# Wide 512-column matmuls for seven query and key chunks, a later load of x and four fewer mask additions

## The reference

```python
def even_layer(x, g_norm, w_in, b_f, w_out):
    z = rms_norm(x, g_norm) @ w_in
    qa, ka, va, ga, fa, qb, kb, vb, gb = jnp.split(z, cuts, axis=-1)
    log_f = jax.nn.log_sigmoid(fa.astype(f32) + b_f.astype(f32))
    ya = forgetting_attention(hA(qa), hA(ka), hA(va), log_f).reshape(Bsz, S, WIDTH_FOX)
    yb = dilated_attention(hB(qb), hB(kb), hB(vb)).reshape(Bsz, S, WIDTH_DIL)
    y = jnp.concatenate([ya * jax.nn.silu(ga), yb * jax.nn.silu(gb)], axis=-1)
    return x + y @ w_out

def odd_layer(x, g_norm, w_in, w_out):
    z = rms_norm(x, g_norm) @ w_in
    q, k, v, g = jnp.split(z, [qk_w, 2 * qk_w, 2 * qk_w + v_w], axis=-1)
    q = rotate(q.reshape(Bsz, S, N_HEADS_RET, RET_QK_DIM))
    k = rotate(k.reshape(Bsz, S, N_HEADS_RET, RET_QK_DIM)) * (RET_QK_DIM ** -0.5)
    y = retention(q, k, v.reshape(Bsz, S, N_HEADS_RET, RET_V_DIM))
```

## Time and profile before

| | us |
|---|---|
| median of 3 runs | 771.15 (771.01 to 771.21) |
| the profiled execution | 770.69 |
| its span, first to last instruction | 768.9 |
| PE busy | 760.5 (99%) |
| DVE busy | 517.2 (67%) |
| ACT busy | 409.8 (53%) |
| POOL busy | 223.6 (29%) |
| DMA moved | 132.01 MB, mean 172 GB/s |

### The profile page before, as it was taken

How to read it: one execution, slowest core, us unless ns; L and a number is a source line. 1 busy time by engine, 2 the same in 40 slices (tenths; PEclk the granted TensorE clock), 3 DMA queues, 4 the chain that set the end, 5 groups by cost and what they waited for, 6 DMA issues and landing times.

```text
span 768.9 us, 12573 instructions
## 1 busy us (share of the span) xinstructions
PE 760.5 (99%) x5026; PEld 658.3 (86%) x5026; DVE 517.2 (67%) x779; ACT 409.8 (53%) x664; POOL 223.6 (29%) x176
## 2 busy tenths in 40 slices
PE   9999999999999999999999999999999999999997
PEld 8889987899877899987778888988888888888885
DVE  5876756665577558765567965778788676667553
ACT  6674458443696453353344554727857555456451
POOL 2110996730940000064029900126012111011010
PEclk9999999999999999999999999999999999999999
DMA  9999893588512746555435565430465556655751
GB/s 284 220 233 301 245 248 65 131 174 198 156 62 80 242 138 194 186 169 159 142 110 164 191 218 168 140 134 30 164 193 152 183 175 204 194 179 175 242 169 55
DMA packets 78490, 132.01 MB, mean 172 GB/s; under 512 B 4592, under 2 KB 28304, under 8 KB 78304
## 3 DMA queue, kind: packets, MB, share of 16 engines
q1 hardware_dynamic: 76928, 126.01, 55.7%
q0 software_dynamic: 1216, 5.09, 2.3%
q10 hardware_dynamic: 288, 0.11, 0.1%
HBM read 130.12 MB, written 1.06 MB: 171 GB/s over the span
## 4 chain that ended last, share of the span: by engine, by line
PE 97%; DVE 1%; ACT 1%; issue 0%; DVEq 0%; ACTq 0%
PE ps L1711 15%; PE ps L1715 15%; PE ps L1719 15%; PE ps L1769 10%; PE ps L1752 6%; PE ps L1756 6%; PE ps L1748 6%; PE ps L1777 5%; PE ps L1839 2%; PE ps L1855 2%; PE ps L1870 2%; PE ps L2225 1%; PE ps L2102 1%; PE ps L2054 1%; PE ps L2110 1%; PE ps L1799 1%
## 5 line engine op out<-in xcount | busy, mean ns | idle before, releaser
L1032 DVE TENSOR_TENSOR w_lo<-stage,w_hi 128x1024 fp32r<-128x1024 f32 x224 | 293.4, 1332 | 150.9 <-ACT w_hi L667 150.2
L667 ACT ACTIVATE w_hi<-stage 128x1024 fp32r<-128x1024 f32 x230 | 239.1, 1060 | 234.1 <-PE ps L1719 104.8
L1711 PE MATMUL ps<-w_hi,act_t 128*128 128x512 f32 (+1 forms) x368 | 100.5, 396 | 0.2 <-ACT act_t L694 0.2
L1719 PE MATMUL ps<-w_lo,act_t 128*128 128x512 f32 (+1 forms) x368 | 96.5, 385 | 0.0
L1769 PE MATMUL ps<-act_t,w_hi 128*128 128x512 f32 x352 | 84.1, 391 | 0.0
L1719 PEld LDWEIGHTS ps<-w_lo,act_t 128*128 128x128 f32 x368 | 68.1, 188 | 14.0
L1711 PEld LDWEIGHTS ps<-w_hi,act_t 128*128 128x128 f32 x368 | 66.5, 188 | 15.1 <-issue 2.5
L1715 PE MATMUL ps<-w_hi,act_t 128*128 128x512 f32 (+1 forms) x304 | 79.4, 384 | 0.0
L1769 PEld LDWEIGHTS ps<-act_t,w_hi 128*128 128x128 f32 x352 | 64.7, 188 | 12.6
L1715 PEld LDWEIGHTS ps<-w_hi,act_t 128*128 128x128 f32 x304 | 56.1, 188 | 11.6
L1748 PE MATMUL ps<-act_t,w_hi 128*128 128x256 f32 x416 | 58.8, 284 | 0.0
(11 more groups left out here) (384 smaller groups left out, 1153.1 us busy)
## 6 DMA issues: line engine op xcount, KB each, us to landing
stage<-in_even_w_in SPq DMA_DIRECT2D x62, 512.0 KB, 5.4
stage<-in_odd_w_in SPq DMA_DIRECT2D x48, 512.0 KB, 3.9
stage<-in_w_gate_up SPq DMA_DIRECT2D x44, 512.0 KB, 4.8
stage<-in_w_down SPq DMA_DIRECT2D x22, 512.0 KB, 4.7
stage<-in_even_w_out SPq DMA_DIRECT2D x16, 512.0 KB, 3.8
stage<-in_odd_w_out SPq DMA_DIRECT2D x16, 512.0 KB, 3.8
stage<-in_w_in SPq DMA_DIRECT2D x10, 512.0 KB, 3.7
stage<-in_w_out SPq DMA_DIRECT2D x8, 512.0 KB, 4.5
```

The source lines that it names most:

```text
L667: nc.scalar.activation(w_hi[:, u % RING, :], stage[:, u % RING, :], ACT.Copy).then_inc(hi_ready, 1)
L1032: nc.vector.tensor_tensor(w_lo[:, u % RING, :], stage[:, u % RING, :], w_hi[:, u % RING, :].bitcast(F32), ALU.subtract).then_inc(lo_ready, 1)
L1711: mm(out[:, b, :], a_hi(k)[:, tok[b]], hi[:, i, :], start=(k == 0), stop=False)
L1719: ins = mm(out[:, b, :], a_hi(k)[:, tok[b]], lo[:, i, :], start=False, stop=(k == k_tiles - 1))
```

## The change

Seven chunks (`WIDE`: qa 0, qa 1, ka 0, ka 1, rq 1, rk 0, rk 1) run as `wide_channels_unit`: a 512-column matmul moves the upper and the lower part of a tile of x at once against the upper weight, and then a 256-column one the upper part against the lower weight. The result takes four banks, whose halves are to be added: ACT copies the second halves to the destination (`take_lower`), DVE adds the first halves and then multiplies or rotates. qb, kb, rq 0 and u stay as they were. Waits are added on PE: before qa 0 for ga 1's drain, before qa 1 for `f_abs`, before rk 0 for a row. The lag products stand in bank 4 instead of 7, behind a wait for rk 0's drain, and retention head 0 waits for their copy, not head 1.

Further: x by tokens is loaded at unit 40 instead of 30; GpSimd doesn't add the mask of the far keys, which is zero everywhere; the change of sign of `c_both` moves on DVE from behind qa 1's drain to behind the first attention's scores.

```diff
-MASKS_AT, X_AT, TABLES_AT = 20, 30, 42
+MASKS_AT, X_AT, TABLES_AT = 20, 40, 42
...
+        WIDE = {("qa", 0): (0, 1, 2, 3), ("qa", 1): (4, 5, 6, 7), ("ka", 0): (0, 1, 2, 3), ("ka", 1): (4, 5, 6, 7),
+                ("rq", 1): (2, 3, 6, 7), ("rk", 0): (0, 1, 4, 5), ("rk", 1): (2, 3, 6, 7)}
...
-                then(nc.gpsimd.tensor_tensor(forget_bias[:, hs, P:S], forget_bias[:, hs, P:S], near, ALU.add))
-                far = neg_bias[:, 0, 0:P].unsqueeze(1).to_broadcast([P, 4, P])
-                nc.gpsimd.tensor_tensor(forget_bias[:, hs, 0:P], forget_bias[:, hs, 0:P], far, ALU.add).then_inc(forget_bias_ready, 1)
+                nc.gpsimd.tensor_tensor(forget_bias[:, hs, P:S], forget_bias[:, hs, P:S], near, ALU.add).then_inc(forget_bias_ready, 1)
...
+            def take_lower(name, dst):
+                ahead(name)
+                chunk_done(act, name)
+                for pair in range(2):
+                    nc.scalar.activation(dst[pair], wide_parts(name, pair)[1], ACT.Copy).then_inc(lower_out, 1)
...
+                if (name, c) in WIDE:
+                    out = [dst[:, 4 * c + 2 * pair:4 * c + 2 * pair + 2, :] for pair in range(2)]
+                    for pair in range(2):
+                        dve.wait_ge(lower_out, 2 * wide_names.index((name, c)) + pair + 1)
+                        TT(out[pair], wide_parts((name, c), pair)[0], out[pair], ALU.add).then_inc(parts_added, 1)
+                    for pair in range(2):
+                        dve.wait_ge(parts_added, 2 * wide_names.index((name, c)) + pair + 1)
+                        ins = TT(out[pair], out[pair], row[:].unsqueeze(1).to_broadcast([P, 2, S]), ALU.mult)
...
+                if half == 0:
+                    dve.wait_ge(c_in_landed, 16)
+                    TS(c_both[:, 1, :], c_both[:, 1, :], -1.0, None, ALU.mult).then_inc(c_ready, 1)
...
+            def wide_channels_unit(name, j, k_tiles, columns, there=always):
...
+                for i, k in enumerate(ks):
...
+                    for m in range(4):
+                        mm(bank(WIDE[name][m]).rearrange("p (v n) -> p v n", v=2), columns(hi[:, i, :], m), both[:, :, k, :], start=(k == 0), stop=False,
+                           skip_group_check=True)
+                lower_there(name, j)
+                for i, k in enumerate(ks):
+                    for m in range(4):
+                        ins = mm(bank(WIDE[name][m], S), columns(lo[:, i, :], m), act_t[:, k, :], start=False, stop=(k == k_tiles - 1), skip_group_check=True)
+                ins.then_inc(unit_used, 1)
...
+            chunk_drained(pe, ("ga", 1))
             channels(("qa", 0))
+            pe.wait_ge(f_abs, 1)
             channels(("qa", 1))
...
+            channels(("rq", 1), pairs)
+            pe.wait_ge(row_taken, 2)
+            channels(("rk", 0), pairs)
+            channels(("rk", 1), pairs)
             pe.wait_ge(c_pow_ready, 3)
+            chunk_drained(pe, ("rk", 0))
...
-                if h == 1:
+                if h == 0:
                     pe.wait_ge(lag_copied, 4)
```

More of the change, by code:

```diff
@@ L320, in ffn_turned_at, with wide_parts @@
             return (4, 2, 5, 3)[k] * BANK if k < 4 else 4 * BANK + k * S
+        WIDE = {("qa", 0): (0, 1, 2, 3), ("qa", 1): (4, 5, 6, 7), ("ka", 0): (0, 1, 2, 3), ("ka", 1): (4, 5, 6, 7),
+                ("rq", 1): (2, 3, 6, 7), ("rk", 0): (0, 1, 4, 5), ("rk", 1): (2, 3, 6, 7)}
+        wide_names = list(WIDE)
+        def wide_parts(name, pair):
+            at = WIDE[name][2 * pair] * BANK
+            both = ps[:, at:at + 2 * BANK].rearrange("p (m v n) -> p m v n", m=2, v=2)
+            return both[:, :, 0, :], both[:, :, 1, :]
         def chunk_done(eng, name):
@@ L806, in copy_prob_act @@
                 nc.scalar.activation(prob_slots[:, n % SLOTS, :], bank(turned_at(n), 384), ACT.Copy).then_inc(prob_copied_act, 1)
+            def take_lower(name, dst):
[3 more added lines that the diff above has]
+                    nc.scalar.activation(dst[pair], wide_parts(name, pair)[1], ACT.Copy).then_inc(lower_out, 1)
+            heads_of_chunk = lambda dst, c: [dst[:, 4 * c + 2 * pair:4 * c + 2 * pair + 2, :] for pair in range(2)]
+            for kind, dst in (("qa", q0), ("ka", k0)):
+                for c in range(2):
+                    take_lower((kind, c), heads_of_chunk(dst, c))
             for half in range(2):
@@ L854, in _ @@
             out_and_turn("even_out", 1, KD + 8, COL_ODD)
-            for kind, n in (("rq", 2), ("rk", 2)):
-                for c in range(n):
-                    ahead((kind, c))
+            for kind, dst in (("rq", q1), ("rk", k1)):
+                for c in range(2):
+                    if (kind, c) in WIDE:
+                        take_lower((kind, c), [dst[:, 2 * c + hh] for hh in range(2)])
+                    else:
+                        ahead((kind, c))
             act.wait_ge(lag_done, 1)
@@ L1324, in _ @@
                     ahead((kind, c))
+                    wide = (kind, c) in WIDE
+                    for hh in range(2):
+                        if wide:
+                            both, count = dst[:, 2 * c + hh], 2 * wide_names.index((kind, c)) + hh + 1
+                            dve.wait_ge(lower_out, count)
+                            TT(both, wide_parts((kind, c), hh)[0], both, ALU.add).then_inc(parts_added, 1)
                     chunk_done(dve, (kind, c))
@@ L1757, in channels_unit @@
                 ins.then_inc(unit_used, 1)
+            def wide_channels_unit(name, j, k_tiles, columns, there=always):
+                hi, lo = unit_of(name, j)
+                both = act_t[:, :, :].rearrange("p (v k) n -> p v k n", v=2)
+                ks = range(2 * j, 2 * j + 2)
+                for i, k in enumerate(ks):
+                    there[0](k)
+                    there[1](k)
+                    for m in range(4):
[6 more added lines that the diff above has]
+                ins.then_inc(unit_used, 1)
             def ffn_two_units(name, first, there=always, between=None):
@@ L1791, in channels @@
                 for j in range(chunks[name][1]):
-                    channels_unit(name, j, KD, columns, there)
+                    if name in WIDE:
+                        wide_channels_unit(name, j, KD, columns, there)
+                    else:
+                        channels_unit(name, j, KD, columns, there)
             def after_lo(count):
```

15 lines of the change are left out of this document (8 added, 7 removed).

## The result

| | before | after |
|---|---|---|
| median | 770.9 us (770.33 to 771.55, 20 executions) | 774.15 us (769.2 to 779.96, 20 executions) |
| the profiled execution | 770.69 us | 770.27 us |
| its span | 768.9 us | 768.4 us |

The ratio is 1.0048, with a 95% interval of 1.0029 to 1.0067: slower by about 3.3 us, where 768.4 was forecast. The executions of before lie within 1.2 us. Those of after form three groups, and the mean granted clock goes with them: five at 769.2 to 770.5 (0.998 to 1.0), seven at 772.0 to 774.3 (0.995 to 0.997), eight at 777.7 to 780.0 (0.994 to 0.996). The profiled one is of the first group, so the profile of after shows how the time is lost, but not all of it. The first experiment, the same kernel again, has a profile of a slower execution.

The account below looks back on a forecast made before the run. PE, busy 99% of the span, was taken as the bound: 2.7 us less from PE and 0 from the rest, off the median of 771.15, gave 768.4 us (80%); range 767.4 to 770.3.

Parts of the forecast that it names:

- PE's gain: Wide units in seven chunks: 2.78 us instead of 2.88, 0.097 saved a unit, 28 units, 2.7 us.
- the bounds of 1.6 to 3.0: PE's saving: low if each of 56 changes of form costs 0.02 us, high at the token matmuls' 227 ns.
- The rule of the Trainium skill: Start to start is columns at 2.4 GHz plus about 2.5 ns: 0.6 us saved on 224 pairs, time 770.6.
- it holds: In ka 0 and ka 1 lower halves lead PE by 4.4 us; the longer drain takes 1.3 to 2.1.
- rival 2: DVE falls behind in ka 0 and ka 1: chunk 15.0 us against PE's 11.1, PE waits 3.4, time 771.8; 6%.
- would charge the new SBUF multiplications too: GpSimd's lock of a shared port, against DVE operations with two SBUF inputs, would also slow the drain's multiplications; no size given.
- Covered by 2 us: With x behind unit 39, exponents of heads 2 and 3 end near 121; PE turns the first at 122.9.
- the third rival: Loads behind x delay unit 42 to 126, exponents of heads 2 and 3 late: 774.5 us; 3% slower, 4% within 0.2%.
- GpSimd and c_both: Four additions fewer, about 7.8 us of GpSimd, worth nothing on the path; moved sign nothing, or 0.6 us uncovered.
- some 8 us earlier the stretch in which DVE is slow: Dropping GpSimd's four mask additions was to end DVE's slow stretch beside it that much sooner; worth nothing on the path.
- The signs: Error would show as a wide group nearer 1.92 us, PE waiting for a drain, or heads 2 and 3 turned late.
- the first two rivals: Wide switch buys nothing, 512-column matmul 240 ns, 771.15 us, 7%; DVE behind in ka 0 and ka 1, 771.8, 6%.

Follow-up runs that it names:

- the repeat: The changed kernel measured once more with no edit: median 776.8 us, ratio 1.0069; its profiled execution took 777.66 us.
- The sum in PSUM: Changed kernel, but DVE writes the sum of the two halves back into PSUM and multiplies from there: 769.71 us, ratio 0.9982.
- the additions back: Changed kernel with GpSimd's four additions of the far mask put back: 775.78 us, ratio 1.0062.
- the broadcast later: Changed kernel with GpSimd's 2 MB broadcast of cum_forget issued only after unit 26 has landed: 772.99 us, ratio 1.0026.

## Why the prediction was wrong

**PE's gain.** The mechanism was right, its size a little off. In qa and ka the unit fell to 2.79 to 2.80 us as forecast (2.78): 1.4 us measured for 16 units, 1.6 forecast. In the 12 units of retention it was 2.83, 0.7 us instead of 1.2, because there the stationary operand is read with a stride, which the forms of the feed-forward that I priced by do not have. Together 2.1, inside the bounds of 1.6 to 3.0. The rule of the Trainium skill (TensorE: Matmul & The Clock Gate, Back-to-back issue gap), by which 0.6 us would have been gained, does not hold here: eight matmuls of 256 columns take 0.95 to 0.96 us, 119 ns each, and eight of 512 take 1.84, 230 ns. The section gives that rule for an isolated matmul, and about 131 ns at 512 columns for a stream of weight loads and matmuls; these rows agree with neither.

**The step that failed** is "it holds", the lead of 4.4 us in ka 0 and ka 1. Its working charged the longer drain with 1.3 to 2.1 us, and that once, and left the lower halves at 1.98 each. Measured in the repeat: the two multiplications 2.38 to 3.04 us instead of at most 2.1, the four lower halves 9.00 and 8.52 instead of 7.91, a chunk 12.7 instead of the 11.3 that rival 2 gives for measured durations. That is 1.5 us behind for every chunk, over three drains (qa 1, ka 0, ka 1), where the rival counted two. It is not the same in every execution: in the faster one of the result the second cycle took 9.5 us, its four lower halves 6.25, beside a GpSimd as busy. What makes the difference was not tested; it does not come from the edits, for the kernel is the same. The sum in PSUM shows that the second SBUF operand is what makes the drain slow and most of the loss: 1.27 us, 7.91 us, 10.2 us a chunk, and 769.7 instead of 774 to 777. The control stands in the trace of after as well: qa 0's multiplications, at 66.09, before GpSimd's additions, took 1.27 us for two, qa 1's 2.37.

The prediction had the sentence that says so: the Trainium skill (SBUF — State Buffer, SBUF: two separate sides) "would charge the new SBUF multiplications too". I wrote it and did not put it through the sum. The trace agrees with the page: 2.4 to 3.0 us against 1.27 for a pair. I priced a single operation beside GpSimd by the mean of others, and took the engine's rows for independent, while a shift of one against the other changed the lower halves as well (7.91 to 9.00).

**The start of the stretch** I did not see at all. The lead was read from before, where unit 26 landed ahead of the broadcast. There SP issued its load at 64.21, and GpSimd the broadcast at 65.68 us. The change brings the two together: after has the broadcast at 65.00 and the load at 64.99, and ACT converts the unit at 75.57, where it did at 72.38. With wide chunks in retention alone the order is that of before (64.21 and 65.69). An order between queues that rests on 1.5 us is no part of a lead that can be counted on. With the sum in PSUM and x at 50 it is nevertheless harmless.

**x at unit 40.** "Covered by 2 us" was right for an SP queue on time (the kernel before with x at 40: no loss) and wrong for one held back by VectorE. SP issues unit u behind the lower half of unit u - 4, so the lag of VectorE and the transfer of x add up in front of unit 42. In the profile of after that unit landed at 120.6, between the 117.2 that I had worked out and the 124 of the third rival, "landings at 120 to 123 eat part of the gain". Rivals 2 and 3 were priced apart, at 6 and 7%; they are one chain, the first brings on the second, and only together do they give the time. x back at 30 or on to 50 takes 4 to 5 us off the repeat's median on that chip.

**GpSimd and c_both.** Forecast at nothing by themselves; nothing measured speaks against it. But that the additions left out end "some 8 us earlier the stretch in which DVE is slow" was misread: GpSimd goes on with other work at once, and the four lower halves from 103.33 on are slow too (6.24 for the first three). So the edit gave back nothing of the lead that could be shown.

**The clock.** No step spoke of what a single wait sets off. In the slower executions a wait of about 3 us costs another 1.6 to 1.8 at the lower level. It is why the loss is larger than the waits.

**The signs.** Of the three that I had named one appeared: the probabilities of heads 2 and 3 are turned late. A wide group near 1.92 did not, and neither did a wait of PE for a drain; in its place the repeat has waits for the lower halves that are queued behind the drains. The range ended at 770.3 because it took in about half of each of the first two rivals (no gain, VectorE behind), each alone, and nothing of the third.

## What to carry to other kernels

When a drain is split into a copy by one engine and an addition by another, leave the running value in PSUM until the last operation. An operation of VectorE with both inputs in SBUF had no fixed price beside a busy GpSimd here, and it made its neighbours dearer too. Work the queue of the engine out for the whole cycle that repeats, each form at its worst row, and compare it with PE's cycle; a lead is spent per chunk. And where one delay holds back the queue on which a second risk depends, price the two together.

## What the runs showed of the hardware

After a wait of 3 us PE ran at half clock for part of the next 4 us, in the repeat, with the additions back and with the broadcast later, and so it did after one of 2.2 us (ka 0 and ka 1 narrow). After the waits of 1.7 us or less in the profiles of after, x at 50, x at 30 and the sum in PSUM it stayed at 1.00. With the broadcast later (PE alone: busy, granted clock, DMA share, GB/s):

```profile
124.00:126.00 2.00, 0.00 (x0) 1.00 1.05 181
126.00:128.00 2.00, 1.78 (x10) 0.51 0.96 171
128.00:130.00 2.00, 2.00 (x14) 0.64 0.11 37
```

The 2 MB broadcast delays one or two unit loads by 4 to 5 us, and which ones is decided by about 1 us in the order of two queues.

Eight 512-column matmuls with a strided stationary operand took 1.86 to 1.89 us, with a plain one 1.84. The narrow groups behind them took 0.95 to 0.96 in both.

Beside GpSimd the same two 128x512 multiplications of VectorE took 1.27 us from PSUM and 2.1 to 3.2 us from SBUF; from SBUF ahead of GpSimd's additions they took 1.27.
